# Seven-product pairs of a decoder trunk: ring slots, load order, turned rows, and products of gate and up on VectorE

## The reference

```python
D_MODEL = 1024
D_FF = 3584
def swiglu(h, w_gate, w_up, w_down):
    return (jax.nn.silu(h @ w_gate) * (h @ w_up)) @ w_down
...
hn = rms_norm(h, ffn_norm[layer])
h = h + swiglu(hn, dense_w_gate[e], dense_w_up[e], dense_w_down[e])
```

## Time and profile before

| | |
|---|---|
| Median of 3 runs | 1503.91 us (1501.05 to 1504.5) |
| Profiled execution | 1502.78 us, span 1501.0 us |
| Mean granted TensorE clock | 0.996 |
| TensorE busy | 1472.6 us, 98% |
| VectorE busy | 1252.3 us, 83% |
| ScalarE busy | 976.9 us, 65% |
| GpSimd busy | 154.6 us, 10% |
| Chain that ended last | TensorE 87%, issue 5%, DMA 3%, VectorE 2%, GpSimd 2% |

### The profile page before, as it was taken

One profiled execution on the slowest core, in us unless ns is written; L12 is line 12 of the kernel. 1 busy time (PEld: TensorE's weight loads), 2 busy tenths in 40 slices (PEclk: granted clock), 3 DMA queues, 4 the chain that ended last, 5 costly groups with the idle time before them and its releaser, 6 DMA issues.

```text
span 1501.0 us, 20262 instructions
## 1 busy us (share of the span) xinstructions
PE 1472.6 (98%) x7852; PEld 1229.2 (82%) x7852; DVE 1252.3 (83%) x1091; ACT 976.9 (65%) x873; POOL 154.6 (10%) x103
## 2 busy tenths in 40 slices
PE   9999999898999999999999999999999999999998
PEld 7899987787887788888888888888888888888886
DVE  5977766788978789889889898898898988988985
ACT  4455535465556567777777687776777677767673
POOL 0480120011212000000000000000000000000000
PEclk9999999999999999999999999999999999999999
DMA  8568779565462399999999999999999999999990
GB/s 281 169 174 220 282 141 374 174 235 187 158 240 96 152 348 393 397 381 395 396 382 393 391 374 380 385 369 380 382 383 369 391 382 361 392 383 359 395 362 30
DMA packets 195561, 466.58 MB, mean 311 GB/s; under 512 B 6060, under 2 KB 6352, under 8 KB 195499
## 3 DMA queue, kind: packets, MB, share of 16 engines
q1 hardware_dynamic: 184656, 434.31, 77.7%
q0 software_dynamic: 10352, 30.98, 8.2%
q10 hardware_dynamic: 490, 0.42, 0.1%
HBM read 458.86 MB, written 24.67 MB: 322 GB/s over the span
## 4 chain that ended last, share of the span: by engine, by line
PE 87%; issue 5%; DMA 3%; DVE 2%; POOL 2%; ACT 1%; SPq 0%; DVEq 0%; POOLq 0%; ACTq 0%
PE bank L1803 14%; PE bank L1805 14%; PE bank L1804 14%; PE bank L1788 7%; PE bank L1790 7%; PE bank L1789 7%; PE bank L935 4%; PE bank L1022 2%; DMA ring<-in_a_w_in 2%; PE bank L1026 1%; PE bank L1027 1%; PE bank L1028 1%; PE bank L1496 1%; POOL xbuf L865 1%; DMA ring<-in_dense_w_gate 1%
## 5 line engine op out<-in xcount | busy, mean ns | idle before, releaser
L3099 DVE TENSOR_TENSOR ring_r<-ring,buf_r 128x2048 fp32r<-128x2048 f32 x336 | 751.4, 2285 | 28.0 <-ACT buf_r L2301 28.0
L2301 ACT ACTIVATE buf_r<-ring 128x2048 fp32r<-128x2048 f32 x336 | 629.3, 1914 | 51.3 <-PE bank L1790 43.4
L1803 PE MATMUL bank<-ring_r,buf_r 128*128 128x512 f32 x896 | 354.8, 396 | 0.3 <-DVE buf_r L3219 0.3
L1805 PE MATMUL bank<-buf_r,buf_r 128*128 128x512 f32 x896 | 349.9, 390 | 0.0
L1804 PE MATMUL bank<-buf_r,buf_r 128*128 128x512 f32 x896 | 349.2, 390 | 0.0
L1805 PEld LDWEIGHTS bank<-buf_r,buf_r 128*128 128x128 f32 x896 | 168.2, 188 | 35.8
L1804 PEld LDWEIGHTS bank<-buf_r,buf_r 128*128 128x128 f32 x896 | 168.6, 188 | 33.4
L1803 PEld LDWEIGHTS bank<-ring_r,buf_r 128*128 128x128 f32 x896 | 168.5, 188 | 33.5 <-DVE buf_r L3219 0.4
L1788 PE MATMUL bank<-ring_r,buf_r 128*128 128x512 f32 x440 | 173.0, 393 | 0.1
L1790 PE MATMUL bank<-buf_r,buf_r 128*128 128x512 f32 x440 | 171.6, 390 | 0.0
L1789 PE MATMUL bank<-buf_r,buf_r 128*128 128x512 f32 x440 | 171.3, 389 | 0.0
(11 more groups left out here) (411 smaller groups left out, 2037.2 us busy)
## 6 DMA issues: line engine op xcount, KB each, us to landing
ring<-in_moe_w_gate SPq DMA_DIRECT2D x56, 2048.0 KB, 10.1
ring<-in_moe_w_up SPq DMA_DIRECT2D x56, 2048.0 KB, 10.6
ring<-in_moe_w_down SPq DMA_DIRECT2D x56, 2048.0 KB, 10.4
ring<-in_a_w_in SPq DMA_DIRECT2D x8, 2048.0 KB, 9.9
ring<-in_dense_w_down SPq DMA_DIRECT2D x14, 1024.0 KB, 5.2
ring<-in_dense_w_gate SPq DMA_DIRECT2D x12, 1024.0 KB, 12.6
ring<-in_dense_w_up SPq DMA_DIRECT2D x12, 1024.0 KB, 7.2
weight_sums<-in_dense_w_gate POOLq DMA_DIRECT2D x8, 1024.0 KB, 8.7
```

The lines of the kernel that those rows point to most:

```text
L1803: pe.matmul(o, xh, low[:, c], start=k == 0, stop=False)
L1805: ins = pe.matmul(o, xh, high[:, c], start=False, stop=k == KT - 1)
L2301: act.activation(HB[m % NHB], half_words(m, U_MOE), ACT.Copy).then_inc(m_wh, 1)
L3099: dve.tensor_tensor(half_low(m, U_MOE), half_words(m, U_MOE), HB[m % NHB], ALU.subtract).then_inc(m_wl, 1)
```

## The change

It alters tables and places in the queues; the arithmetic of the output is the same.

- Blocks 6 to 11 get ring slots 3, 6 and 5 instead of 1, 2 and 4 (a second time). Their loads wait for `o_mm` or `wo_mm`, semaphores of the stage before, instead of `d_used`. Blocks 12 to 17 keep slots 3, 6 and 5, now as second users, and wait for `d_used` 7 to 12.
- `turns_after` for pair 1 is 12, 14, 16, 18 (was 12, 13, 15, 16) and for pair 2 is 28, 31, 33, 35 (was 28, 30, 31, 32); pair 3 keeps 46, 48, 49, 50. ScalarE and VectorE take up a turned piece at m = turn + 4 instead of + 5.
- The three products per seven-product pair move from GpSimd to VectorE (`piece_hidden`), one at m = s + 8 and two at s + 10 of the up quad. Waits on `quad_p` for them become waits on `pr_ready`; the turns take the pieces in the order (0,0), (1,1), (1,0), (0,1).
- The silus and products of the plain pair come in twos: at + 5, + 5, + 7, + 7 instead of + 5, + 6, + 7, + 8.
- GpSimd's DMAs: the second half of `sums_start(0)` and both `sums_add(0, ...)` come one level of masks later; `sums_add(1, 2)` and `sums_add(1, 3)` wait for `d_used` 10 and 12.

```diff
     s = pair_at(p, "up")
     if p in PLAIN:
-        return [s + 2, s + 3, s + 5, s + 6]
-    return [s + 5, s + 7, s + 8, s + 9]
+        return [s + 2, s + 4, s + 6, s + 8]
+    return [s + 5, s + 8, s + 10, s + 12] if p < PAIRS else [s + 5, s + 7, s + 8, s + 9]
...
-    return 2 * TT + sum(4 if i in PLAIN else 1 for i in range(1, p))
...
+    return 2 * TT + 4 * (p - 1)
+
+
+def hidden_turn(p, sl, t):
+
+    order = [(0, 0), (0, 1), (1, 0), (1, 1)] if p in PLAIN else [(0, 0), (1, 1), (1, 0), (0, 1)]
+    return hiddens_before(p) + order.index((sl, t)) + 1
...
-    return DSLOTS[n if n < SHORT else (n - SHORT) % 6], m % 2
+    return DSLOTS[n if n < 6 else (n - SHORT) % 6], m % 2
...
                         sp.wait_ge(vn_mm, 2)
-                    elif m < NB - 2 and block_before(m) < 0:
+                    elif m < 8:
+                        sp.wait_ge(o_mm, 4)
+                    elif m < 12:
                         sp.wait_ge(wo_mm, 4)
                     elif m < NB - 2:
                         sp.wait_ge(d_used, block_before(m) + 1)
...
                 if lv == 3:
-                    sums_add(0, 0)
+                    sums_start(0, [2, 3])
...
-                    sums_add(0, 1)
+                    sums_add(0, 0)
+            sums_add(0, 1)
...
-            sums_add(1, 2)
-            sums_add(1, 3)
+            for qd in (2, 3):
+                pool.wait_ge(d_used, pair_at(1, "up") + 2 * (qd - 2))
+                sums_add(1, qd)
...
-            both_parts(1)
-            quad_hidden(MIXED[0])
-            both_parts(2)
-            both_parts(3)
-            quad_hidden(MIXED[1])
+            for qd in range(1, QUADS):
+                both_parts(qd)
...
+            def piece_hidden(qd, i):
+
+                p = quad_pair(qd)
+                sl, t = ((1, 1), (1, 0), (0, 1))[i]
+                dve.wait_ge(part_v, 4 * qd + 2 + i)
+                dve.wait_ge(sg_ready, silus_before(p) + 2 + i)
+                dve.tensor_tensor(QPR[:, sl, t, :], QPR[:, sl, t, :], QSG[:, sl, t, :], ALU.mult).then_inc(pr_ready, 1)
...
-                        if m == after + 5:
+                        if m == after + 4:
                             hidden_low(2 * p - 1 + g // 2, g % 2)
...
+                    if qd % 2 == 1 and m == s + 8:
+                        piece_hidden(qd, 0)
+                    if qd % 2 == 1 and m == s + 10:
+                        for i in (1, 2):
+                            piece_hidden(qd, i)
...
-                        if m == pair_at(p, "up") + 5 + i:
+                        if m == pair_at(p, "up") + 5 + i // 2 * 2:
                             plain_hidden(p, i // 2, i % 2)
```

More of the change, by code:

```diff
@@ L810, in _ @@
             sums_start(0, [0, 1])
-            landed(pool, 2)
             def proj_low(f):
@@ L821, in _ @@
             proj_low(6)
-            sums_start(0, [2, 3])
             for g in range(4):
@@ L857, in both_parts @@
                 pool.tensor_tensor(out, out, FIRSTP, ALU.add).then_inc(quad_p, 1)
[L859 to L866, removed]
             both_parts(0)
@@ L1325, in hidden_tp @@
                     pe.wait_ge(ht_ready, 2 * j + t)
[L1326 to L1331, removed]
+                    pe.wait_ge(pr_ready, hidden_turn(p, 1 - j % 2, t))
                 src = FPR[:, t, :] if j == 0 else QPR[:, 1 - j % 2, t, :]
@@ L1396, in quad_products @@
                 elif p > 1:
-                    pe.wait_ge(pr_ready, hiddens_before(p) - (p - 1 in PLAIN))
+                    pe.wait_ge(pr_ready, hiddens_before(p) - (1 if p - 1 in PLAIN else 3))
                 product(m, A_BANK, rows_of(0, 0), start=True)
@@ L1414, in quad_products @@
                 product(m + 4, B_BANK, mixed(2))
+                hidden_turns(m + 4)
                 pe.wait_ge(first_out, 2 * qd + 2)
@@ L2111, in first_part @@
                     act.wait_ge(part_v, 4 * qd)
-                    act.wait_ge(quad_p, pool_part(qd - 1))
+                    act.wait_ge(quad_p, qd)
                 act.activation(FIRSTP, as_quad(A_BANK), ACT.Copy).then_inc(first_out, 1)
@@ L2118, in fifth_part @@
                 act.wait_ge(d_used, quad_at(qd) + 3)
-                if qd % 2 == 0 and p - 1 in PLAIN:
+                if qd % 2 == 0:
                     act.wait_ge(pr_ready, hiddens_before(p))
-                elif qd % 2 == 0 and p > 1:
-                    act.wait_ge(quad_p, pool_hidden(p - 1, 3))
                 act.activation((QPR if qd % 2 else QSG)[:, 1, 1, :], bk[C_BANK][:, :], ACT.Copy).then_inc(first_out, 1)
@@ L2141, in plain_silu @@
                     act.wait_ge(pr_ready, hiddens_before(p))
-                    if p > 1 and p - 1 in MIXED:
-                        act.wait_ge(quad_p, pool_hidden(p - 1, 3))
                 act.activation(QSG[:, sl, t, :], bk[PLAIN_BANK["gate"][sl][t]][:, :], ACT.Silu).then_inc(sg_ready, 1)
@@ L2177, in _ @@
                     for i in range(4):
-                        if m == pair_at(p, "gate") + 5 + i:
+                        if m == pair_at(p, "gate") + 5 + i // 2 * 2:
                             plain_silu(p, i // 2, i % 2)
@@ L2823, in sixth_part @@
                 dve.wait_ge(first_out, 2 * qd + 1)
-                if qd % 2 == 0 and quad_pair(qd) - 1 in MIXED:
-                    dve.wait_ge(quad_p, pool_hidden(quad_pair(qd) - 1, 3))
+                if qd % 2 == 0:
+                    dve.wait_ge(pr_ready, hiddens_before(quad_pair(qd)))
                 dve.tensor_tensor(as_blocks(quad_out(qd)[:, 1, 0, :]), as_quad(B_BANK), FIRSTP, ALU.add).then_inc(part_v, 1)
@@ L2837, in last_piece @@
                 o = quad_out(qd)[:, 1, 1, :]
-                dve.wait_ge(quad_p, pool_part(qd))
+                dve.wait_ge(quad_p, qd + 1)
                 dve.wait_ge(d_used, quad_at(qd) + 5)
```

## The result

The changed kernel takes 1517.34 us (median of 4 runs, 1517.15 to 1517.49) against 1503.12 us of the kernel before, measured beside it: a ratio of 1.0096, with a 95% interval of 1.0078 to 1.0113. It is slower by 14 us. The profiled execution took 1517.15 us, its span is 1515.3, so the difference between the two profiled executions is 14.4 us.

What follows compares the result with a forecast made beforehand. TensorE, busy 98% of the span, was taken to bound the kernel; +32.0 + 1.6 - 12.6 - 4.6 = +16.4 us on 1502.78 gave 1519.2, stated as 1519.5 us, range 1504 to 1530.

Steps and rivals of the forecast that it cites:

- The stall: TensorE stands inside block 12, 267.6 to 299.6, because loads of blocks 17 to 19 come late: 32.0 us.
- the sum: Stall's timing: block 11 ends 264.9, block 19 lands 290; VectorE's second sum, two copies, fourth sum and product end 299.6.
- Its two halves: Late loads alone stall block 12 for 17.6 us, adds beside them lengthen it; undisturbed loads as rival: 1504.8 us, chance 0.12.
- The lower clock after it: Behind the stall in block 12, about 8 slow TensorE products: 1.6 us.
- The six waits: TensorE's dense-stage waits over 0.5 us, 12.6 us in sum, plus 4.6 us of slow products, all gone.
- the sixth: Wait of 0.73 us for a turn needing GpSimd's product; gone with the product on VectorE.
- First: Wait of 2.79 us behind block 6's late gate load; new free slots remove it and 1.6 us of slow products.
- Second: Wait of 2.44 us at product 15; pair 1's product moved ahead of a weight copy removes it and 1.4 us.
- Third and fifth: Turns waiting 1.80 and 1.78 us for VectorE's low half; spaced turns and halves a block earlier win 3.6 us.
- Fourth: Turn waiting 3.05 us for GpSimd's 2.3 us product; on VectorE it takes 0.68, winning 3.05 + 1.6 us.
- The rest at nothing: Later first-pair sums on GpSimd, a possibly later input-projection load and shifted silus were put at no cost or gain.
- The price of three more products per pair on VectorE: VectorE gains 2.0 us of work per pair, hidden under TensorE: net nothing; the two pairs could cost up to 4 us.

Runs made afterwards that it cites:

- e2_adds_early: Changed kernel with the second pair's adds issued at once, as before the change: 1500.81 us, 0.9992 of the kernel before.
- e3_only_slots: Kernel before with only the change's ring slots and load waits, adds early: 1515.67 us, 1.0087 of the kernel before.
- e1_slots_back: Changed kernel with the ring slots and load waits of before, late adds kept: 1482.06 us, 0.9864 of the kernel before.
- f1_turns_back: Kernel of e1_slots_back with the turns of before, products on VectorE, halves still at turn + 4: 1486.49 us, 0.9899 of the kernel before.
- g2_halves_back: Kernel of e1_slots_back with halves of turned pieces at turn + 5 again, turns as in the change: 1482.26 us, 0.9869 of the kernel before.
- f2_gpsimd: Kernel of e1_slots_back with three products per seven-product pair on GpSimd again, turns as in the change: 1482.03 us, 0.9867 of the kernel before.
- f3_18_first: Changed kernel with loads of blocks 18 and 19 issued right behind 13: 1498.71 us, 0.9977 of the kernel before.
- f4_adds_later: Kernel of e1_slots_back with the second pair's adds waiting for d_used 14 and 16, not 10 and 12: 1486.36 us, 0.9893 of the kernel before.
- e4_only_early: Kernel before with only GpSimd's copies and adds of the first pair's sums a mask level later: 1497.87 us, 0.9979 of the kernel before.

## Why the prediction was right

The forecast was 1519.5 us, the measured time is 1517.3; slower, by the mechanism that was named. Point by point:

- *The stall, 32.0 us.* Measured 33.46. The chain behind the landing took the 9.6 us of the sum (287.52 to 297.14). The landing came 26.5 us after block 11's end, the sum had 25.1. The 1.4 us lie in the stretch in which the adds, the copy for normed rows and four loads share the DMA engines; which of its terms was too small is open.
- *Its two halves.* With the adds away the bound was 17.6 us; run e2_adds_early shows 17.83.
- *The lower clock after it, 1.6 us.* 12 products instead of 8: 2.4 us. They fill 5.3 us (297.20 to 302.48), where the prediction had TensorE back at the full clock after some 3.3. The text had said that no row shows this.
- *The six waits, 12.6 and 4.6 us.* Gone, but for 0.18 us of the sixth. The sum was right, the reasons only in part. First: by e3_only_slots the slots take it away as predicted, but by e1_slots_back the late adds do so without them. Second: given to the product's new place ahead of a copy. No run tries that place alone; with the old turns and early halves (f1_turns_back) product 15 finds its input, but the product before it waits 2.00 us. Third and fifth: I gave them to the room between turns together with the halves' place; by f1_turns_back the place alone removes them, though at the price of that wait of 2.00 us, and by g2_halves_back the room alone leaves 0.9 us of them. Fourth: given to the products' move from GpSimd. By f2_gpsimd the turn's new place wins it with the products left on GpSimd, and by f1_turns_back the move alone leaves 2.48 of 3.05 us. The step that fails is "on VectorE the same shape takes 0.68": the product's own duration was not what TensorE waited for, but its turn in a full queue.
- *"The rest at nothing".* Wrong by 3.9 us, the one term that was put at nothing and was not: I found no wait of TensorE behind the first pair's copies because I looked where the adds went (100 to 135 us), not where the copies came from. ScalarE's wait of 3.98 us for a load at 76 us was in the trace.
- *The price of three more products per pair on VectorE.* Nothing, as said: 0.18 us of TensorE's time is idle from 300 to 440 us.

The balance: 33.5 + 2.4 + 0.2 - 17.2 - 3.9 = 15.0 us, against 14.4 between the profiled executions; 0.6 us stay unassigned. The errors had opposite signs, 1.5 + 0.8 + 0.2 up and 3.9 down. The mechanism of the stall was foreseen; that the total came within 2.2 us is in part luck.

## What to carry to other kernels

A queue in order turns one late wait into a wait for everything behind it, however long its places have been free: when slots are given to blocks anew, list for each load which event now releases it, and then which loads stand behind it. When a change moves slots, turns, products and copies at once, try its parts one by one. Here the slots cost 35 us and hid that the other parts together were worth 1.4%, and that the move of the products, priced at 5.4 us (3.05 + 1.6 + 0.73), was worth about 1 us where the turns have moved too. Two queues at work moved as many packets each, so an add that nobody waits for cut the loads beside it to a third of their speed; put such a transfer where no load is waited for.

## What the runs showed of the hardware

- Accumulating transfers between DRAM tensors moved 0.207 MB/us alone, loads 0.383. Together each queue gets the same number of packets (655 and 656 in 10 us), 0.131 MB/us each: a load runs at a third of its speed. The Trainium skill (DMA: Bandwidth & Descriptors, Queues, rings and completion order) has the turns by packets; the trace agrees.
- How long TensorE stays at the lower clock after a wait does not follow from the wait's length alone: 12 slow products after 33.46 us, 10 after 17.74 (e3_only_slots), 7 after 17.83 (e2_adds_early), 9 after 15.83 (f3_18_first), and none after the 2.57 us of f4_adds_later (its granted clock in 300 to 320 us is 1.00, below), though 2.44 us had cost 7 in the kernel before. Nor does the clock always fall before TensorE starts again: behind the 2.42 us of e3_only_slots it fell after six products, behind a wait of 3.14 us in e4_only_early after three.
- The clock differs between executions of one kernel too. Beside the experiments the kernel before took from 1496.92 us, at a mean granted clock of 0.999, to 1504.99 at 0.992. The 4.6 us of slow products in the prediction are those of the one profiled execution.

The stretch of f4_adds_later:

```profile
300.00:320.00 20.00, 17.57 (x77) 14.56 (x78) 19.97 (x12) 14.25 (x11) 1.30 (x1) 1.00 1.06 337
```
